# A decoder layer with retrieved experts: how many expert rows are gathered per group, and where two steps stand in their queues

## The chip, the cores and the metric

The kernel runs as one program on one NeuronCore of a Trainium2 chip. The metric is the device time of one execution in microseconds (us), the median of several runs. The engines are TensorE (PE, its weight loads PEld), VectorE (DVE), ScalarE (ACT), GpSimd (POOL) and SyncE (SP). Each runs its own queue in order. Engines wait for one another through semaphores, and transfers run on 16 DMA engines.

## What is computed

One decoder layer over 1024 tokens of width 1024. After RMSNorm, half of the heads run dilated-window attention and half run latent attention; their output is projected and added. Then comes the part that the change touches, a mixer over 16384 single-neuron experts:

```python
def peer(hn, w_pq, sub_keys, u_emb, v_emb):
    q = (t @ w_pq).reshape(-1, 8, 2, 128)
    sc = einsum('thpc,hpnc->thpn', q, sub_keys)
    vals, idx = top_k(sc, 16)                       # ranking
    cand = vals[:, :, 0, :, None] + vals[:, :, 1, None, :]
    best, flat = top_k(cand.reshape(..., 256), 16)
    expert = i1 * 128 + i2                          # 8 heads x 16 experts per token
    gate = softmax(best)
    act = gelu(einsum('td,thkd->thk', t, u_emb[expert]))
    out = einsum('thk,thkd->td', act * gate, v_emb[expert])
```

The layer's output is the final RMSNorm of the residual plus `out`.

## The kernel before

The stages follow one another: projection, attention, output projection, then `route` (ranking), `spread_gates` (gate tables) and `run_experts`.

**Two ways for the experts.** 576 tokens are computed densely: every expert's u is multiplied with every token, and the result is gated by a table that is zero where the expert was not chosen. The other 448 tokens are computed by gathering. They form 7 units of 64 tokens. For each unit the u rows of 128 tokens-by-slots are gathered by an indirect DMA into a ring of 4 tiles of 128x1024, and each tile costs one "dot" on DVE. Then v rows are gathered into a ring of 8 tiles. Four tiles make one "row sum" on PE (`sums`, L1921).

**Groups.** `run_experts` walks over 64 groups of two expert chunks each. On PE a group is `activations(g+1, 0)`, the first half of `out(g)`, `activations(g+1, 1)`, the second half of `out(g)`. I call an activation (48 matmuls, L1879) with the output half behind it (48 matmuls, L1895) a **half**. The output half is four fills of PSUM, and each fill needs the fill two before it to have been added to `acc` on DVE (`add`, L2084). 16 of the 128 chunks had their activations computed early, in `route`; chunk n is such a one where n % 8 is 3. So each group g with g % 4 == 0 has no second activation: I call it a **short group**.

**Where the row sums stand.** PE calls `catch_up(rows)` at four places of a group: behind the first activation (a), behind the first output half (b), behind the second activation (c), behind the second output half (d). At each it runs the row sums that the rows up to that number allow: all rows of the groups before, plus none, a quarter, a half, three quarters of this group's new rows, rounded down.

**The table of gathers.** `plan` sets how many dots and v rows each group gets. v rows of a unit may begin in the group after the one in which the unit's 64 dots are known to be done. POOL issues a group's u and v gathers in turn (L1844, L1852). A u gather waits for the dot four before it, a v gather for the row sum that frees its place. Before the change there are 9 dots a group up to group 9, then 8 dots and 8 v rows to group 54, 7 and 8 in group 55, and 80 v rows in groups 56 to 62.

**DVE in a group.** After each activation and its gelu on ACT (L1982), DVE runs `gated` (L2060), `split_u` (L2048), `split_w` (L2065) and then `add(g, 0)` or `add(g, 4)`. In the first half it also runs `split_v` (L2070), which the output half needs.

**Ranking's tail.** `route` goes over 8 heads. Beside the ranking it computes 16 early chunks. Each takes a transfer, a copy on ACT (L1178), a subtraction on POOL (`low`, L1294), 48 matmuls on PE (L1104) and a gelu on ACT (L1184). The last four chunks come with the last head.

Of the kernel before, what the change touches and what calls it, by code (L numbers as in the profile page):

```python
# [34 lines left out]
NC_ = sum(RUN)  # L35
NEXP = NKEY * NKEY
UNITS, UNIT, PIECES = 7, 64, 4
ROWS_A_GROUP, MOST_DOTS, LAST_ROWS = 16, 9, 16
T0 = UNITS * UNIT
TD = SEQ - T0  # L40
GT = (T0 + P - 1) // P
# [4 lines left out]
PER_HEAD, U_BUFS = 2, 2  # L46
# [937 lines left out]
def route(core, hn_hi, hn_lo, w_raw, keys, slotT, eid, eidT, sgate):  # L984
# [15 lines left out]
    with ExitStack() as ctx:  # L1000
# [172 lines left out]
        def _(act):  # L1173
            def copy_u(k):
                act.wait_ge(u_in, ONE + k * 16 + 16)
                if k >= U_BUFS:
                    act.wait_ge(act_done, ONE + k + 1 - U_BUFS)
                nc.scalar.activation(u_hi[:, k % U_BUFS, :], u_raw[:, :], ACT.Copy).then_inc(u_hi_ready, 1)  # L1178
# [63 lines left out]
            first_head()  # L1242
            for h in range(1, PH):
                head(h)
            k = 6 * PER_HEAD
            copy_u(k)
            copy_u(k + 1)
            gelu(k)
            gelu(k + 1)
            exponentials(PH)  # L1250
            copy_u(k + 2)
            copy_u(k + 3)
            gelu(k + 2)
            gelu(k + 3)
            for m in range(2):
                act.wait_ge(gelu_sent[m], ONE + 16 * PRE // 2)
            act.wait_ge(eidT_done, 1)
# [28 lines left out]
        @block.gpsimd  # L1286
        def _(pool):
            own = Own(pool, own_p)

            def low(k):  # L1290
                pool.wait_ge(u_hi_ready, ONE + k + 1)
                if k >= U_BUFS:
                    pool.wait_ge(act_done, ONE + k + 1 - U_BUFS)
                nc.gpsimd.tensor_tensor(u_lo[:, k % U_BUFS, :], u_raw[:, :], u_hi[:, k % U_BUFS, :].bitcast(f32), ALU.subtract  # L1294
                                        ).then_inc(u_lo_ready, 1)

            for h in range(PH):
                k = (h - 1) * PER_HEAD
                for j in range(PER_HEAD if h else 0):
                    low(k + j)  # L1300
                pool.wait_ge(keys_ranked, ONE + h + 1)
                pool.wait_ge(found_ready, ONE + h * NQ)
                near_sums(nc.gpsimd, own)
                pair_sums(nc.gpsimd, own, number, top_key)
                pool.sem_inc(number_ready, 1)
                for q in range(NQ):
                    n = h * NQ + q
                    pool.wait_ge(hit_ready, ONE + n * 2 + 2)
                    pool.wait_ge(summed, ONE + n * 2)
                    for z, src in ((0, near), (1, number)):  # L1310
                        own.mark(nc.gpsimd.tensor_tensor(
                            founds[z][:, :, :, :], hits[z][:, q % 2, :, :, :],
                            src[:, q * QT:(q + 1) * QT, :].rearrange("p i (c o) -> p i c o", o=1)
                            .to_broadcast([P, QT, (NN, NC_)[z], HALF]), ALU.mult))
                    own.sync()
                    pool.sem_inc(found_ready, 1)
                for j in range(PER_HEAD, 4 if h == PH - 1 else 0):
                    low(k + j)
                own.restart()

        @block.vector
# [132 lines left out]
class Lead:  # L1454
# [17 lines left out]
    def copy_u(self, nc, act, c):  # L1472
        act.wait_ge(self.u_in[c], 16)
        nc.scalar.activation(self.u_hi[:, c, :, :], self.u_raw[:, c, :].rearrange("p (j e) -> p j e", e=P),
                             ACT.Copy).then_inc(self.u_hi_ready, 1)
# [142 lines left out]
def plan(groups):  # L1618

    total = UNITS * UNIT
    turn, wrote = [], []
    u_by, v_by = [0], [0]
    while v_by[-1] < total:
        g, u, v = len(u_by), u_by[-1], v_by[-1]
        if len(turn) < UNITS and u >= (len(turn) + 1) * UNIT and len(wrote) >= PIECES * len(turn):
            turn.append(g)
        ready = min(sum(UNIT for t in turn if t < g) - v, UNIT - v % UNIT)
        nv = min(ready, LAST_ROWS if u == total and v % UNIT else 8)  # L1630
        nu = min(total - u, ROWS_A_GROUP - nv, MOST_DOTS)
        while len(wrote) * (UNIT // PIECES) < v + nv:
            wrote.append(g)
        u_by.append(u + nu)
        v_by.append(v + nv)
    spare = groups - len(u_by)
    assert spare >= 0
    return u_by + [total] * spare, v_by + [total] * spare, turn, wrote


def run_experts(core, eid, eidT, sgate, lead):
# [21 lines left out]
    with ExitStack() as ctx:  # L1663
# [378 lines left out]
        def _(dve):  # L2042
# [126 lines left out]
            for g in range(NG):  # L2169
# [7 lines left out]
                    coefficients(x)  # L2177
                some_dots(g, 2, 3)
                gated(g + 1, 0)
                split_u(g + 2, 0)  # L2180
                split_w(g + 1, 0)
                for x in closes(g):
                    close(x)
                add(g, 0)
                some_dots(g, 3, 4)
                add(g, 1)
                add(g, 2)
                some_dots(g, 4, 5)
                add(g, 3)
# [1 line left out]
                    take_coef(g, x)  # L2191
                some_dots(g, 5, 7)
                gated(g + 1, 1)
                split_u(g + 2, 1)
                split_w(g + 1, 1)
                for x in closes(g - 1):
                    mean(x, False)
                add(g, 4)
                some_dots(g, 7, 8)
                add(g, 5)  # L2200
                add(g, 6)
                some_dots(g, 8, 9)
                for x in closes(g - 2):
# [108 lines left out]
```

## Time and profile before

| | |
|---|---|
| median of 3 runs | 3306.6 us (3303.07 to 3311.08) |
| profiled execution | 3305.81 us, its span 3304.0 us |
| PE busy | 2975.8 us, 90% |
| DVE busy | 2220.1 us, 67% |
| POOL busy | 1264.4 us, 38% |
| ACT busy | 988.9 us, 30% |
| mean granted TensorE clock | 0.972 of full speed |

`run_experts` begins near 1399 us and is more than half of the span. The share of busy time of an engine is a mean over stages, so the stages have to be read one by one. Matmul ends are modelled in the trace; the starts of PE's instructions are what a length is taken from. The profiled execution lies 0.8 us below the median.

### The profile page before, as it was taken

The page shows a single profiled execution, that of the slowest core. Times are in us where ns is not written, and L with a number is a line of the kernel's source. Part 1 is how long each engine was busy: PE and PEld are TensorE (multiplying, and loading weights), DVE is VectorE, ACT ScalarE, POOL GpSimd, SP SyncE. Part 2 cuts the span into 40 slices and gives each one's busy share as a digit, 9 for nine tenths or more (in the row PEclk, how much of TensorE's full clock was granted, in tenths as well). Part 3 has the DMA queues.
Part 4 walks back from the last instruction along what each step waited for, and adds up shares of the span by engine and source line. Part 5 has one row for each costly group of instructions (what it writes and reads, how often), then busy time and mean ns, then how long its engine had stood idle before and what let it go on. Part 6 is the DMA issues. An engine that isn't in the chain of part 4 may idle for free.

```text
span 3304.0 us, 52758 instructions
## 1 busy us (share of the span) xinstructions
PE 2975.8 (90%) x19914; PEld 2435.1 (74%) x19914; DVE 2220.1 (67%) x5340; ACT 988.9 (30%) x1452; POOL 1264.4 (38%) x1088
## 2 busy tenths in 40 slices
PE   8997988997898666689999999999999999999997
PEld 4444666545777566688888888888889889888876
DVE  2223544336999889868887777778777777777435
ACT  2223655312222278722221222221222221222212
POOL 0000000001343400023357767767677666675241
PEclk9998999999999899999999999999999999999998
DMA  5213111112121126798799999999999999999684
GB/s 190 99 62 120 40 42 36 35 57 99 62 69 43 47 64 191 245 302 269 256 325 387 379 377 382 390 371 389 382 381 380 380 386 378 379 387 338 227 320 167
DMA packets 330177, 779.26 MB, mean 236 GB/s; under 512 B 45649, under 2 KB 147281, under 8 KB 328529
## 3 DMA queue, kind: packets, MB, share of 16 engines
q0 software_dynamic: 129024, 469.82, 37.8%
q1 hardware_dynamic: 178512, 288.92, 25.0%
q10 hardware_dynamic: 22400, 17.32, 1.6%
q8 instruction: 150, 2.46, 0.3%
q14 instruction: 91, 0.74, 0.1%
HBM read 699.42 MB, written 72.35 MB: 234 GB/s over the span
## 4 chain that ended last, share of the span: by engine, by line
PE 45%; DVE 9%; DMA 5%; issue 3%; ACT 1%; POOL 1%; SPq 0%; DVEq 0%; ACTq 0%
PE psum L1879 21%; PE psum L1895 19%; PE psum L1921 5%; DVE first L1564 4%; DMA u_ring<-u_rows,eid 3%; DVE one L1557 1%; DMA scr_g<-gates 1%; DVE acc L2084 1%; DVE u_lo L2048 1%; POOL v_ring L1852 1%; ACT u_hi L1976 1%; DVE second L1567 1%; DMA v_ring<-v_rows,eidT 1%; DMA v_raw<-v_rows 0%; DVE w_lo L2065 0%
## 5 line engine op out<-in xcount | busy, mean ns | idle before, releaser
L1852 POOL DMA_INDIRECT v_ring<-v_rows,eidT x448 | 598.2, 1335 | 413.0 <-PE psum L1921 303.4
L1844 POOL DMA_INDIRECT u_ring<-u_rows,eid x448 | 513.1, 1145 | 293.4 <-DVE dots L2092 187.7
L2092 DVE CUSTOM_DVE_ANT_0 u_ring<-u_ring,rows 128x1024 f32<-128x1024 f32 x448 | 545.0, 1218 | 98.1 <-DMA u_ring<-u_rows,eid 97.2
L1879 PE MATMUL psum<-hn_hi_e,u_hi 128*128 128x288 f32 x1792 | 531.2, 296 | 8.5 <-SPq L108 5.0
L1879 PE MATMUL psum<-hn_lo_e,u_hi 128*128 128x288 f32 x1792 | 528.8, 295 | 0.0
L1879 PE MATMUL psum<-hn_hi_e,u_lo 128*128 128x288 f32 x1792 | 528.5, 295 | 0.0
L1895 PE MATMUL psum<-w_hi,v_hi 128*128 128x288 f32 x2048 | 464.9, 309 | 69.6 <-DVE acc L2084 59.0
L2084 DVE TENSOR_TENSOR acc<-psum,acc 128x576 f32<-128x576 f32 x504 | 380.1, 755 | 138.8 <-PE psum L1895 128.5
L1895 PEld LDWEIGHTS psum<-w_hi,v_hi 128*128 128x128 f32 x2048 | 333.9, 193 | 171.0 <-issue 91.0
L1895 PE MATMUL psum<-w_lo,v_hi 128*128 128x288 f32 x2048 | 446.8, 300 | 0.0
L1895 PE MATMUL psum<-w_hi,v_lo 128*128 128x288 f32 x2048 | 446.1, 300 | 0.0
L1879 PEld LDWEIGHTS psum<-hn_hi_e,u_hi 128*128 128x128 f32 x1792 | 338.2, 189 | 14.9 <-issue 14.9
L1895 PEld LDWEIGHTS psum<-w_hi,v_lo 128*128 128x128 f32 x2048 | 338.2, 193 | 0.0
L1895 PEld LDWEIGHTS psum<-w_lo,v_hi 128*128 128x128 f32 x2048 | 338.1, 193 | 0.0
L1879 PEld LDWEIGHTS psum<-hn_lo_e,u_hi 128*128 128x128 f32 x1792 | 338.0, 189 | 0.0
L1879 PEld LDWEIGHTS psum<-hn_hi_e,u_lo 128*128 128x128 f32 x1792 | 337.6, 188 | 0.0
L1982 ACT ACTIVATE psum<-psum 128x576 f32<-128x576 f32 x112 | 71.1, 635 | 872.1 <-PE psum L1879 872.1
L1993 ACT ACTIVATE v_hi<-v_raw 128x1024 fp32r<-128x1024 f32 x128 | 128.8, 1054 | 407.4 <-PE psum L1895 395.7
L2060 DVE TENSOR_TENSOR w<-psum,w 128x576 f32<-128x576 f32 x112 | 84.8, 757 | 232.3 <-ACT psum L1982 219.6
L1921 PE MATMUL psum<-v_ring,strip 128*32 128x512 f32 x1792 | 216.9, 602 | 10.4 <-DMA v_ring<-v_rows,eidT 10.4
L473 PE MATMUL psum<-w_in,hT 128*128 128x512 f32 (+1 forms) x512 | 211.7, 575 | 0.0
L1582 PE MATMUL psum<-second,first 128*128 128x128 f32 x1152 | 148.0, 283 | 70.7 <-DVE second L1567 70.7
(238 smaller groups left out, 4192.8 us busy)
## 6 DMA issues: line engine op xcount, KB each, us to landing
v_raw<-v_rows SPq DMA_DIRECT2D x128, 512.0 KB, 7.1
u_raw<-uT SPq DMA_DIRECT2D x112, 512.0 KB, 8.1
w<-scr_g SPq DMA_DIRECT2D x128, 288.0 KB, 5.8
scr_g<-gates SPq DMA_DIRECT2D x3, 8192.0 KB, 30.6
scr_m<-st_m SPq DMA_DIRECT2D x8, 1024.0 KB, 4.0
w_raw<-in_w_pq SPq DMA_DIRECT2D x8, 1024.0 KB, 6.6
u_raw_r<-uT SPq DMA_DIRECT2D x16, 512.0 KB, 3.5
scr_g<-gates ACTq DMA_DIRECT2D x1, 7680.0 KB, 36.9
```

Of the source, the lines that this page charges most:

```text
L473: last = nc.tensor.matmul(ps[:, 2 + c, 0:width(c)], hT[:, k, j, :], w_in[:, j, c * BANK:c * BANK + width(c)], start=j == 0, stop=j == KD - 1)
L1564: nc.vector.tensor_scalar(first[:, b, t, :], iota_f[:, :], flat[:, 0, at:at + 1], flat[:, 2, at:at + 1], ALU.is_equal, ALU.mult).then_inc( ...
L1582: last = nc.tensor.matmul(slot, first[:, b, t, :], second[:, b, t, :], start=True, stop=True)
L1844: pool.indirect_dma_start(u_ring[:, n % U_RING, :], None, core.i["u_rows"], bass.IndirectOffsetOnAxis(eid[:, x // 2, x % 2, k:k + 1], 0)). ...
L1852: pool.indirect_dma_start(v_ring[:, m % V_RING, :], None, core.i["v_rows"], bass.IndirectOffsetOnAxis(eidT[:, x // 2, col:col + 1], 0)).th ...
L1879: last = nc.tensor.matmul(ps[:, a, 0:COLS], x[:, c, j, :], y[:, j, a * COLS:(a + 1) * COLS], start=m == 0, stop=m == len(terms) - 1)
L1895: last = nc.tensor.matmul(ps[:, OUT_AT + F % OUT_PAIRS * 2 + a, 0:COLS], x[:, c, f * P:(f + 1) * P], y[:, b, c, a * COLS:(a + 1) * COLS], ...
L1921: last = nc.tensor.matmul(ps[k * WIDE:(k + 1) * WIDE, SUM_AT + half, :], strip[:, p % 2, at:at + WIDE], v_ring[:, n % V_RING, half * BANK: ...
L1993: nc.scalar.activation(v_hi[:, c, :], v_raw[:, c, :], ACT.Copy).then_inc(v_hi_ready, 1)
L2060: nc.vector.tensor_tensor(half, ps[:, 0:ACTS, 0:COLS], half, ALU.mult).then_inc(w_ready, 1)
L2084: nc.vector.tensor_tensor(into, ps[:, at:at + 2, 0:COLS], into, ALU.add).then_inc(added, 1)
L2092: nc.vector.tensor_tensor_reduce(out=u, in0=u, in1=rows[:, x % 2, :], scale=1.0, scalar=0.0, op0=ALU.mult, op1=ALU.add, accum_out=dots[:, ...
```

## The change

The table of gathers becomes: 10 dots a group in groups 1 to 8; then 8 dots with 7 v rows (8 in the first group of each unit's v rows) in groups 9 to 54; then, with no dots left, 16 v rows a group, 120 of them in groups 55 to 62. In groups whose predecessor has no v rows (0 to 9), `add(g, 0)`, `add(g, 1)`, `add(g, 4)` and `add(g, 5)` move ahead of `split_w`, the first of each pair ahead of `split_u`. In `route` POOL runs the last four `low` in a row ahead of the last head's `near_sums`, and ACT runs its last four chunks ahead of the last head's exponentials.

```diff
-ROWS_A_GROUP, MOST_DOTS, LAST_ROWS = 16, 9, 16
+U_ROWS, MOST_DOTS, LAST_ROWS = 8, 10, 16
...
-            k = 6 * PER_HEAD
-            copy_u(k)
-            copy_u(k + 1)
-            gelu(k)
-            gelu(k + 1)
+            copy_u(6 * PER_HEAD)
+            copy_u(6 * PER_HEAD + 1)
+            for k in range(6 * PER_HEAD, PRE):
+                gelu(k)
+                if k + 2 < PRE:
+                    copy_u(k + 2)
             exponentials(PH)
-            copy_u(k + 2)
-            copy_u(k + 3)
-            gelu(k + 2)
-            gelu(k + 3)
...
-                for j in range(PER_HEAD if h else 0):
+                for j in range(0 if h == 0 else PER_HEAD if h < PH - 1 else PRE - k):
                     low(k + j)
...
-                for j in range(PER_HEAD, 4 if h == PH - 1 else 0):
-                    low(k + j)
...
-        nv = min(ready, LAST_ROWS if u == total and v % UNIT else 8)
-        nu = min(total - u, ROWS_A_GROUP - nv, MOST_DOTS)
+        nv = min(ready, LAST_ROWS if u == total else 7 if v % UNIT else 8)
+        nu = min(total - u, U_ROWS if nv else MOST_DOTS)
...
                 gated(g + 1, 0)
+                alone = not g or v_by[g - 1] == 0
+                if alone:
+                    add(g, 0)
                 split_u(g + 2, 0)
+                if alone:
+                    add(g, 1)
                 split_w(g + 1, 0)
                 for x in closes(g):
                     close(x)
-                add(g, 0)
+                if not alone:
+                    add(g, 0)
                 some_dots(g, 3, 4)
-                add(g, 1)
+                if not alone:
+                    add(g, 1)
```

The second half of a group is changed in the same way, with `add(g, 4)` and `add(g, 5)`.

On PE, group 11 before: a row sum (L1921) stands between each activation (L1879) and its output half (L1895).

```order
L1879 MATMUL psum<-hn_hi_e,u_hi 128x288
...
L1921 MATMUL psum<-v_ring,strip 32x512 x8
L1895 MATMUL psum<-w_hi,v_hi 128x288 x2
...
L1879 MATMUL psum<-hn_hi_e,u_hi 128x288
...
L1921 MATMUL psum<-v_ring,strip 32x512 x8
L1895 MATMUL psum<-w_hi,v_hi 128x288 x2
...
```

Group 11 now (L1874, L1916 and L1890 are the same three statements):

```order
L1874 MATMUL psum<-hn_hi_e,u_hi 128x288
...
L1890 MATMUL psum<-w_hi,v_hi 128x288 x2
...
L1916 MATMUL psum<-v_ring,strip 32x512 x8
L1874 MATMUL psum<-hn_hi_e,u_hi 128x288
...
L1890 MATMUL psum<-w_hi,v_hi 128x288 x2
...
L1916 MATMUL psum<-v_ring,strip 32x512 x8
```

Both row sums moved behind the output half. With 7 rows a group the quarter points fall differently in each of four groups, and a group has one of these four forms (a, b, c, d as above, the number of row sums at each):

| form | a, b, c, d | ordinary groups among 11 to 54 | short groups among them |
|---|---|---|---|
| P | 1, 0, 0, 1 | 7 | 2 |
| Q | 0, 1, 0, 1 | 8 | 2 |
| R | 0, 0, 1, 0 | 6 | 4 |
| S | 1, 0, 1, 0 | 12 | 3 |

Before the change all 44 of these groups have form S.

On DVE, the first half of a group without v rows, before: three steps and then the first addition.

```order
L2060 TENSOR_TENSOR w<-psum,w 128x576
L2048 TENSOR_TENSOR u_lo<-u_raw,u_hi 128x1024
L2065 TENSOR_TENSOR w_lo<-w,w_hi 128x576
L2084 TENSOR_TENSOR acc<-psum,acc 128x576
L2092 ISA u_ring,dots<-u_ring,rows 128x1024
```

And now:

```order
L2055 TENSOR_TENSOR w<-psum,w 128x576
L2079 TENSOR_TENSOR acc<-psum,acc 128x576
L2043 TENSOR_TENSOR u_lo<-u_raw,u_hi 128x1024
L2079 TENSOR_TENSOR acc<-psum,acc 128x576
L2060 TENSOR_TENSOR w_lo<-w,w_hi 128x576
```

The two additions moved ahead, one of them past two steps.

On POOL, the last head before: two subtractions, the sums of the last head, and two subtractions at the end.

```order
L1294 TENSOR_TENSOR u_lo_r<-u_raw_r,u_hi_r 128x1024 x2
L1281 TENSOR_TENSOR near<-top_key 128x8x8
...
L1311 TENSOR_TENSOR found<-hit,near 128x640
L1311 TENSOR_TENSOR found<-hit,number 128x1600
L1294 TENSOR_TENSOR u_lo_r<-u_raw_r,u_hi_r 128x1024 x2
L93 ISA
```

And now all four stand ahead of the sums:

```order
L1291 TENSOR_TENSOR u_lo_r<-u_raw_r,u_hi_r 128x1024 x4
L1278 TENSOR_TENSOR near<-top_key 128x8x8
...
L1308 TENSOR_TENSOR found<-hit,near 128x640
L1308 TENSOR_TENSOR found<-hit,number 128x1600
L93 ISA
```

## Rows read from the trace of the kernel before

**Rows 1.** Windows; columns: stretch, length, each engine's busy us, clock, DMA share, GB/s.

```profile
1458.00:1694.00 236.00, 214.23 (x1540) 207.37 (x1539) 195.32 (x289) 50.94 (x64) 93.75 (x79) 0.99 0.80 267
1780.00:3011.00 1231.00, 1200.58 (x8935) 1061.22 (x8935) 953.67 (x1391) 275.97 (x346) 854.10 (x673) 0.98 1.00 381
3011.00:3263.00 252.00, 239.21 (x1800) 202.09 (x1802) 116.33 (x153) 50.87 (x65) 94.40 (x90) 0.99 0.77 280
```

**Rows 2.** Timeline, PE, a half of group 13; columns: start us, us, instruction.

```profile
1780.23 0.29 PE L1879 MATMUL psum<-hn_hi_e,u_hi 128*128 128x288 f32 x1
...
1786.67 1.92 PE L1921 MATMUL psum<-v_ring,strip 128*32 128x512 f32 x16
...
1788.52 0.53 PE L1895 MATMUL psum<-w_hi,v_hi 128*128 128x288 f32 x2
...
1795.03 0.29 PE L1879 MATMUL psum<-hn_hi_e,u_hi 128*128 128x288 f32 x1
```

**Rows 3.** Timeline, PE, the first half of group 10.

```profile
1693.91 0.29 PE L1879 MATMUL psum<-hn_hi_e,u_hi 128*128 128x288 f32 x1
...
1700.27 0.43 PE L1895 MATMUL psum<-w_hi,v_hi 128*128 128x288 f32 x2
...
1704.71 0.53 PE L1895 MATMUL psum<-w_hi,v_hi 128*128 128x288 f32 x2 [1.09 <-DVE acc L2084]
...
1708.20 0.29 PE L1879 MATMUL psum<-hn_hi_e,u_hi 128*128 128x288 f32 x1
```

**Rows 4.** Timeline, DVE, in the same half of group 10.

```profile
1701.21 0.76 DVE L2060 TENSOR_TENSOR w<-psum,w 128x576 f32<-128x576 f32 x1 [1.29 <-ACT psum L1982]
1702.10 1.22 DVE L2048 TENSOR_TENSOR u_lo<-u_raw,u_hi 128x1024 fp32r<-128x1024 f32 x1
...
1703.91 0.75 DVE L2084 TENSOR_TENSOR acc<-psum,acc 128x576 f32<-128x576 f32 x1
```

**Rows 5.** Timeline, PE, group 59, a row sum behind an output half.

```profile
3145.43 1.92 PE L1921 MATMUL psum<-v_ring,strip 128*32 128x512 f32 x16
...
3147.28 0.40 PE L1879 MATMUL psum<-hn_hi_e,u_hi 128*128 128x288 f32 x1
```

**Rows 6.** Timeline, short group 12: POOL, DVE, PE.

```profile
1763.11 0.94 POOL L1844 DMA_INDIRECT u_ring<-u_rows,eid  x1 [0.30 <-issue]
...
1770.99 1.23 DVE L2092 CUSTOM_DVE_ANT_0 u_ring<-u_ring,rows 128x1024 f32<-128x1024 f32 x1 [1.30 <-DMA u_ring<-u_rows,eid]
...
1775.42 0.54 PE L1895 MATMUL psum<-w_hi,v_hi 128*128 128x288 f32 x2 [2.64 <-DVE acc L2084]
```

**Rows 7.** Windows: short group 12, then groups 59, 60 (short) and 61.

```profile
1752.60:1780.20 27.60, 24.96 (x178) 21.52 (x177) 22.95 (x35) 5.86 (x7) 21.26 (x17) 0.94 1.03 408
3130.60:3164.10 33.50, 33.50 (x257) 27.12 (x256) 15.20 (x21) 9.97 (x12) 11.86 (x12) 1.00 0.78 287
3164.10:3199.00 34.90, 28.71 (x212) 21.26 (x208) 15.48 (x19) 6.21 (x8) 16.10 (x16) 0.96 0.99 360
3199.00:3232.90 33.90, 33.90 (x260) 27.48 (x256) 11.96 (x15) 6.11 (x8) 16.21 (x16) 0.99 0.79 285
```

**Rows 8.** Timeline, group 2, dots alone: PE, DVE, PE.

```profile
1472.33 0.29 PE L1879 MATMUL psum<-hn_hi_e,u_hi 128*128 128x288 f32 x1
...
1476.63 1.22 DVE L2070 TENSOR_TENSOR v_lo<-v_raw,v_hi 128x1024 fp32r<-128x1024 f32 x1
...
1478.69 0.43 PE L1895 MATMUL psum<-w_hi,v_hi 128*128 128x288 f32 x2
```

**Rows 9.** Timeline, the end of ranking: POOL, DVE, PE, and DVE's first step of the next stage.

```profile
1123.56 1.64 POOL L1281 TENSOR_TENSOR near<-top_key 128x64 f32<-128x64 f32 x8 [1.42 <-DVEq L1431]
...
1153.58 0.38 DVE L1412 CAST slot<-key_i 128x80 f32<-128x80 int32 x2
...
1164.18 0.60 PE L1163 MATMUL psum<-ident,eid_f 128*128 128x128 f32 x4
...
1172.22 0.69 DVE L1548 CAST iota_gb<-iota 128x1024 bf16<-128x1024 f32 x1 [18.27 <-PEq L108]
```

More of the change, by code:

```diff
@@ L2193, in _ @@
                 gated(g + 1, 1)
+                if alone:
+                    add(g, 4)
                 split_u(g + 2, 1)
+                if alone:
+                    add(g, 5)
                 split_w(g + 1, 1)
@@ L2197, in _ @@
                     mean(x, False)
-                add(g, 4)
+                if not alone:
+                    add(g, 4)
                 some_dots(g, 7, 8)
-                add(g, 5)
+                if not alone:
+                    add(g, 5)
                 add(g, 6)
```

## The prediction

> **What bounds the kernel now.** I read the windows by stage first, because the shares on the page mix them. From 1780 to 3011 us, the stage with dots and v rows, PE is busy 1200.6 of 1231.0 us and the DMA share is 1.00 at 381 GB/s [rows 1]. So two things could set the pace there, and the timeline of PE has to say which. In an ordinary half it runs without a gap: activation from 1780.23, row sum from 1786.67, output from 1788.52, the next activation at 1795.03 [rows 2]. That is 6.44 + 1.85 + 6.51 = 14.80 us, and the half behind it is the same. PE is the bound, not the DMA engines. The number of matmuls is unchanged, so the time can only change through PE's waits.
>
> Where PE waits, it is for DVE's additions. The first half of group 10 has no row sum between activation and output. It takes 1708.20 - 1693.91 = 14.29 us although it has 1.85 us less to do: PE stops 1.09 us ahead of the third fill, and about 0.4 us in smaller stops [rows 3]. The reason is DVE's order: `gated` at 1701.21, `split_u`, `split_w`, and only at 1703.91 the addition that frees the PSUM for the third fill [rows 4]. A row sum ahead of the output half gives DVE just that time. So a row sum there costs 14.80 - 14.29 = 0.5 us, not 1.85. **This is the number on which the forecast rests.** A row sum behind the output half covers nothing: it costs 1.85 us [rows 5], about 1.9 with the slower restart.
>
> The short groups are the exception. Group 12 takes 27.6 us [rows 7] against 6.4 + 4 x 3.25 + 2 x 1.85 = 23.1 of work. Its last two fills wait for DVE: a dot waits 1.30 us for a u row that was issued at 1763.11, and PE's fill comes at 1775.42 after 2.64 us [rows 6]; the mean clock of the group is 0.94 [rows 7]. The eleven short groups among 12 to 52 take 27.9 us on average by the starts of their first activations.
>
> **The dots-alone stage.** It fills 1458 to 1694 us [rows 1]. Each half takes 14.3 us, for the reason of [rows 3]. With the additions ahead, the 1.47 us of waits in a half go, since the addition is done 1.81 us earlier (the span from `split_u` to `add`, 1702.10 to 1703.91) [rows 4]. But the tenth dot takes some of it back. In the first half the output waits for `split_v`: now it ends near 1477.85, and the output starts at 1478.69, 6.36 us after the activation began at 1472.33 [rows 8]. Slack 0.84. One more dot (1.14 from start to start) stands ahead of it, and PE arrives 1.47 sooner relative to DVE: 0.84 - 1.14 - 1.47 = -1.8, a new wait. A group becomes 2 x (6.36 + 6.48) + 1.8 = 27.5 instead of 28.6: -1.1 each in five ordinary groups. The two short groups lose about 1.5 each (the 1.81 of `add(g, 4)` less some lateness). Group 1 loses 1.1, group 9 nothing. Group 10 gets form P: +1.9. Sum: -5.5 - 3.0 - 1.1 + 1.9 = **-7.7**. Bounds: -17 if the tenth dot finds room, +2 if it costs 1.14 in full.
>
> **The mixed stage, groups 11 to 54.** All 44 groups now have form S, and 33 of them are ordinary ones of 29.6 us. By [rows 2, 3, 5]:
> P = 14.8 + 14.3 + 1.9 = 31.0, or +1.4; 7 groups, +9.8.
> Q = 2 x 14.3 + 2 x 1.9 = 32.4, or +2.8; 8 groups, +22.4.
> R = 14.3 + 14.8 = 29.1, or -0.5; 6 groups, -3.
> S = +0; 12 groups.
> Ordinary groups together +29.2. Ten row sums leave this stage for the end, but 23 of those that stay stand where they cover nothing.
>
> In a short group the end is set by DVE, from the first `gated` on. Form R lacks the wait for one row sum's fill (-0.6) and the late u row (-1.3): -1.9. Q and P end with a bare sum, +1.9, less about 0.5 of the dot's wait: +1.4. S is +0.7, as in groups 40 and 44 the sixth u row is queued behind a v row that waits for the sum at a. That is 4 x -1.9 + 4 x 1.4 + 3 x 0.7, or **0**. Bounds: 27.9 could fall to 24.9 if the late row (1.3) and the slow clock (1.7) both went, -33 for the eleven; +2 each, +22. I take 0, as the 1.4 us and more that PE waits for DVE's order stay in all of them, and the clock fell there. Together **+29**.
>
> **The end, groups 55 on.** Before, groups 55 to 62 took 252 us [rows 1]. Now seven of eight have 16 rows. Ordinary: 33.5, or 33.9 behind a short one; short: 34.9, as its row sums wait for the ring of eight [rows 7]. So 3 x 33.5 + 2 x 33.9 + 2 x 34.9 + 29.8 for group 58 and 1.0 for coefficients and a `close` = 268.9: **+17**. Bounds +12 and +22 (the short ones wait 8 us now; 3 more or less each).
>
> **Ranking.** POOL starts the last head's `near_sums` at 1123.56. It now runs two more `low` first. Each waits for a transfer, ACT's copy and PE's chunk before; laid out by the row starts, the fourth ends near 1136.5, so the sums are 13 us later. The exponentials come after the last gelu, near 1147 instead of 1133. From there DVE and POOL need as long as before: the last row on DVE moves from 1153.6 to about 1160.8. But the transposes had waited for PE's last chunk until 1164.18, and that now ends near 1144. Transposes at 1161 let ACT end at 1165. Then SP is last, with eight small transfers (5.4 us to issue, some 2 to land): 1168.4 in place of 1170.6. The next stage starts at 1170 instead of 1172.2 [rows 9]: **-2**. Bounds -5 and +3. If the cover of PE's chunk were gone without the gain, the 7 us on DVE would show.
>
> The first group's gain is swallowed: group 1's output waits for v rows of the dense path that land at a time set by the transfers.
>
> **Sum.** -2 - 7.7 + 29 + 0 + 17 = +36 on a span of 3304.0. The profiled execution is 0.8 below the median, so the median goes from 3306.6 to about **3343 us**.
>
> **Rivals.** (1) The DMA engines set the pace of the mixed stage, and the change makes it *faster*. For it speaks the share of 1.00. 37 of 336 v gathers leave groups 13 to 54, 0.524 MB each (128x1024 f32), 19.4 MB, which at 381 GB/s is 51 us. It decides if PE's halves lengthen or shorten with the gathers. Time: 3306.6 - 51 + 17 - 10 = 3263. Against it: gapless halves of 14.80 us [rows 2], and 408 GB/s in a short group [rows 7], so 381 is no ceiling. The Trainium skill (DMA: Bandwidth & Descriptors, Where 436 GB/s comes from) says that for HBM to SBUF the HBM side, about 358 GB/s a core, binds. By that rule the mixed stage would be bound by its transfers. The rows speak against that figure, at 381 and 408. Chance 0.12.
>
> (2) Fewer gathers make u rows land in time, and the short groups keep the fast clock: -33 in place of 0, 3310 us. Speaks for it: the dot's wait in [rows 6]. Against it: without the 1.30 the fill would still come 1.3 us late. Chance 0.08.
>
> (3) A u row queued behind a v row that waits for a late row sum holds DVE. In form R, u row 7 stands behind the v row that waits for the sum at c. If it lands as late as in [rows 6], 7.9 us after its issue, DVE is 2.1 us late in the next group, ten times: +21, 3364 us. I think that such a row lands sooner, since POOL stood still before it. Chance 0.08.
>
> **Chances and range.** My forecast 0.70, the rest 0.02. Its own range is 3318 to 3366, from the bounds above. With (2) and (3) the range is 3300 to 3372, which leaves out (1). About 0.2%, 6.6 us, is what a measurement can tell from no change. Faster 0.13, same 0.08, slower 0.79.
>
> **What would show it.** Halves of 14.3 us with a wait of about 1.1 for `acc` wherever no row sum stands between activation and output, with v rows under way; a row sum behind an output at 1.85; period of four groups near 119 to 121 us where Q and P stand; groups 55 to 62 at 269; groups of 27.5 in the dots-alone stage. Wrong: bare halves of 13 us in the mixed stage, or ordinary covered halves shorter than 14.8. Then the reading of [rows 3] or the bound is wrong.

## The result, and the profile after

The changed kernel takes 3381.4 us (median of 4 runs, 3375.4 to 3384.0) against 3308.1 us of the kernel before in the same session: 1.022 times as long, 95% interval 1.020 to 1.025. It is slower, as forecast, but by 73 us instead of 36, and 3381 lies above the range, which ended at 3372. The profiled execution has a span of 3380.8 us, 76.8 more than before.

Windows of the changed kernel, by the same stages as [rows 1] (columns as there):

```profile
1448.00:1684.50 236.50, 217.18 (x1584) 211.90 (x1583) 205.02 (x307) 51.53 (x64) 117.72 (x93) 0.99 0.86 298
1776.00:3072.30 1296.30, 1203.79 (x8790) 1061.62 (x8789) 947.94 (x1384) 273.66 (x343) 753.35 (x634) 0.98 0.93 346
3072.30:3338.90 266.60, 255.79 (x1908) 205.76 (x1906) 109.92 (x143) 53.48 (x67) 116.96 (x116) 0.98 0.88 314
```

Groups 13 to 54 take 1296 us instead of 1231, with PE busy for nearly the same time (1204 and 1201 us), and the DMA share fell from 1.00 to 0.93. So PE waits there, and the DMA engines are less busy than before.

From here on I measure a group from the start of its first activation to the next group's. All group times are worked out so, from the timelines of PE.

| stretch, us after minus before | forecast | measured |
|---|---|---|
| ahead of the first changed step | 0 | -4.3 |
| ranking's end | -2 | -3.1 |
| gate tables and groups 0 to 10 | -7.7 | 0.0 |
| groups 11 to 54, ordinary, forms P, Q, R | +29 | +27.5 |
| groups 11 to 54, ordinary, form S | 0 | +21.4 |
| groups 11 to 54, short | 0 | +19.7 |
| groups 55 to the end | +17 | +15.6 |
| sum | +36 | +76.8 |

So the account is right where it rests on measured halves. It fails in the forms S and short, which I had put at zero, and by 7.7 us in groups 0 to 10. The groups of the costliest kinds, from the page of the kernel before and then of the changed one (line, engine, operation, count; busy us, mean ns; idle us ahead of them, and its releaser):

```profile
L1852 POOL DMA_INDIRECT v_ring<-v_rows,eidT x448 | 598.2, 1335 | 413.0 <-PE psum L1921 303.4
L2092 DVE CUSTOM_DVE_ANT_0 u_ring<-u_ring,rows 128x1024 f32<-128x1024 f32 x448 | 545.0, 1218 | 98.1 <-DMA u_ring<-u_rows,eid 97.2
```

```profile
L1847 POOL DMA_INDIRECT v_ring<-v_rows,eidT x448 | 524.9, 1172 | 556.7 <-PE psum L1916 444.2
L2087 DVE CUSTOM_DVE_ANT_0 u_ring<-u_ring,rows 128x1024 f32<-128x1024 f32 x448 | 544.5, 1219 | 162.7 <-DMA u_ring<-u_rows,eid 161.3
L1890 PE MATMUL psum<-w_hi,v_hi 128*128 128x288 f32 x2048 | 469.4, 311 | 130.8 <-DVE acc L2079 92.1
```

POOL's v gathers wait 141 us longer for row sums, and DVE's dots wait 64 us longer for u rows. These are sums over the whole kernel; in groups 11 to 54 alone, by the timelines, it is 149 and 55 us. There are fewer gathers to make in these groups, and yet they came later.

**A bare half, as forecast.** PE in group 11 of the changed kernel, to be held against [rows 3] and [rows 5]:

```profile
1715.62 0.40 PE L1874 MATMUL psum<-hn_hi_e,u_hi 128*128 128x288 f32 x1
...
1722.08 0.43 PE L1890 MATMUL psum<-w_hi,v_hi 128*128 128x288 f32 x2
...
1726.53 0.53 PE L1890 MATMUL psum<-w_hi,v_hi 128*128 128x288 f32 x2 [1.10 <-DVE acc L2079]
...
1730.11 1.92 PE L1916 MATMUL psum<-v_ring,strip 128*32 128x512 f32 x16
...
1731.97 0.40 PE L1874 MATMUL psum<-hn_hi_e,u_hi 128*128 128x288 f32 x1
```

The half takes 14.49 us with a stop of 1.10, and the row sum behind it 1.86. Form P measured +1.2 a group, Q +2.7, R -0.5 (forecast +1.4, +2.8, -0.5).

**What the forecast missed.** POOL, DVE and PE where group 21 (form R) passes into group 22 (form S):

```profile
2032.30 0.94 POOL L1839 DMA_INDIRECT u_ring<-u_rows,eid  x1 [0.69 <-DVE dots L2087]
2043.13 1.55 POOL L1847 DMA_INDIRECT v_ring<-v_rows,eidT  x1 [9.88 <-PE psum L1916]
2044.98 0.94 POOL L1839 DMA_INDIRECT u_ring<-u_rows,eid  x1 [0.30 <-issue]
2046.23 1.11 POOL L1839 DMA_INDIRECT u_ring<-u_rows,eid  x1 [0.30 <-issue]
```

```profile
2054.36 1.22 DVE L2087 CUSTOM_DVE_ANT_0 u_ring<-u_ring,rows 128x1024 f32<-128x1024 f32 x1 [5.76 <-DMA u_ring<-u_rows,eid]
```

```profile
2060.00 0.50 PE L1890 MATMUL psum<-w_hi,v_hi 128*128 128x288 f32 x2 [2.38 <-DVE v_lo L2065]
2064.08 0.53 PE L1890 MATMUL psum<-w_hi,v_hi 128*128 128x288 f32 x2 [0.66 <-DVE acc L2079]
```

v row 6 waits 9.88 us for the row sum at c. u row 7 stands behind it in POOL's queue and is issued at 2044.98. Its dot starts at 2054.36, 9.4 us later, after DVE has waited 5.76 us for the row. So `split_v` is late, and PE waits 2.38 and 0.66 us. That is the third rival of the prediction, in its own words. I had given it 0.08.

### The profile page after: what moved, and what is told of

The parts are those of the page before. It is cut to its first block, busy times and chain, and to the rows that moved or that the text cites. A ratio compares the mean times of both kernels' runs of the same rounds, so it can differ in the third digit from the quotient of the medians.

```text
span 3380.8 us, 52758 instructions
## 1 busy us (share of the span) xinstructions
PE 2988.7 (88%) x19914; PEld 2434.0 (72%) x19914; DVE 2208.1 (65%) x5340; ACT 990.5 (29%) x1452; POOL 1200.1 (35%) x1088
## 4 chain that ended last, share of the span: by engine, by line
PE 37%; DVE 12%; DMA 8%; issue 4%; POOL 2%; ACT 1%; SPq 0%; DVEq 0%; POOLq 0%; ACTq 0%
PE psum L1874 17%; PE psum L1890 15%; DMA u_ring<-u_rows,eid 5%; PE psum L1916 5%; DVE first L1559 4%; DVE acc L2079 2%; POOL v_ring L1847 2%; DVE one L1552 1%; DVE u_ring L2087 1%; DVE u_lo L2043 1%; DMA scr_g<-gates 1%; DMA v_ring<-v_rows,eidT 1%; ACT u_hi L1971 1%; POOL u_ring L1839 1%; DVE w_lo L2060 1%
## 5 line engine op out<-in xcount | busy, mean ns | idle before, releaser
L1847 POOL DMA_INDIRECT v_ring<-v_rows,eidT x448 | 524.9, 1172 | 556.7 <-PE psum L1916 444.2
L1839 POOL DMA_INDIRECT u_ring<-u_rows,eid x448 | 523.8, 1169 | 310.8 <-DVE dots L2087 202.1
L1890 PE MATMUL psum<-w_hi,v_hi 128*128 128x288 f32 x2048 | 469.4, 311 | 130.8 <-DVE acc L2079 92.1
L1874 PE MATMUL psum<-hn_hi_e,u_hi 128*128 128x288 f32 x1792 | 533.9, 298 | 8.3 <-SPq L108 5.0
L1874 PE MATMUL psum<-hn_lo_e,u_hi 128*128 128x288 f32 x1792 | 528.4, 295 | 0.0
L1874 PE MATMUL psum<-hn_hi_e,u_lo 128*128 128x288 f32 x1792 | 528.1, 295 | 0.0
L1890 PEld LDWEIGHTS psum<-w_hi,v_hi 128*128 128x128 f32 x2048 | 335.6, 194 | 218.8 <-DVE acc L2079 116.9
L1890 PE MATMUL psum<-w_hi,v_lo 128*128 128x288 f32 x2048 | 447.8, 301 | 0.0
L1890 PE MATMUL psum<-w_lo,v_hi 128*128 128x288 f32 x2048 | 447.5, 301 | 0.0
L1874 PEld LDWEIGHTS psum<-hn_hi_e,u_hi 128*128 128x128 f32 x1792 | 337.3, 188 | 42.3 <-issue 42.3
L1890 PEld LDWEIGHTS psum<-w_lo,v_hi 128*128 128x128 f32 x2048 | 339.3, 194 | 0.0
L1890 PEld LDWEIGHTS psum<-w_hi,v_lo 128*128 128x128 f32 x2048 | 338.5, 194 | 0.0
L1874 PEld LDWEIGHTS psum<-hn_lo_e,u_hi 128*128 128x128 f32 x1792 | 337.4, 188 | 0.0
L1874 PEld LDWEIGHTS psum<-hn_hi_e,u_lo 128*128 128x128 f32 x1792 | 337.2, 188 | 0.0
L1916 PE MATMUL psum<-v_ring,strip 128*32 128x512 f32 x1792 | 219.4, 608 | 12.8 <-DMA v_ring<-v_rows,eidT 12.7
```

The source lines that it names most:

```text
L1839: pool.indirect_dma_start(u_ring[:, n % U_RING, :], None, core.i["u_rows"], bass.IndirectOffsetOnAxis(eid[:, x // 2, x % 2, k:k + 1], 0)). ...
L1847: pool.indirect_dma_start(v_ring[:, m % V_RING, :], None, core.i["v_rows"], bass.IndirectOffsetOnAxis(eidT[:, x // 2, col:col + 1], 0)).th ...
L1874: last = nc.tensor.matmul(ps[:, a, 0:COLS], x[:, c, j, :], y[:, j, a * COLS:(a + 1) * COLS], start=m == 0, stop=m == len(terms) - 1)
L1890: last = nc.tensor.matmul(ps[:, OUT_AT + F % OUT_PAIRS * 2 + a, 0:COLS], x[:, c, f * P:(f + 1) * P], y[:, b, c, a * COLS:(a + 1) * COLS], ...
L1916: last = nc.tensor.matmul(ps[k * WIDE:(k + 1) * WIDE, SUM_AT + half, :], strip[:, p % 2, at:at + WIDE], v_ring[:, n % V_RING, half * BANK: ...
```

## Experiments

Each time is the median of 4 to 10 runs, and each ratio is to runs of the kernel before on the same chip (3305 to 3310 us). The profiles are read from one execution each.

### The parts of the change

`table_alone` is the kernel before with the first hunk and the hunk of `plan` alone:

```diff
-ROWS_A_GROUP, MOST_DOTS, LAST_ROWS = 16, 9, 16
+U_ROWS, MOST_DOTS, LAST_ROWS = 8, 10, 16
...
-        nv = min(ready, LAST_ROWS if u == total and v % UNIT else 8)
-        nu = min(total - u, ROWS_A_GROUP - nv, MOST_DOTS)
+        nv = min(ready, LAST_ROWS if u == total else 7 if v % UNIT else 8)
+        nu = min(total - u, U_ROWS if nv else MOST_DOTS)
```

> The kernel before with nothing changed but the table of gathers. It splits the +73 us. In the two traces the ranking's end gives 3 us (of the 10 us that run_experts starts earlier, 4.3 were there before the first changed step), and group 2, dots alone, went from 28.6 to 27.4 us. With the old order of the additions I expect such a group at 28.9 us (14.3 a half, and the tenth dot 0.3 more than the slack of 0.84), so five such groups and two short ones cost some 9 us more than in the changed kernel. Expected: 3381 + 3 + 9, about 3393 us. If the early additions are what hurts, it comes out below 3375.

Measured: 3395.7 us, ratio 1.025 (1.023 to 1.028). `old_table` is the changed kernel with these hunks undone.

> The changed kernel with the table of before (9 dots, then 8 and 8, 80 v rows at the end); ranking's end and the early additions stay. If the table alone costs, this is faster than before: 3 us from ranking; seven ordinary dots-alone groups at 2 x (6.36 + 6.48) + 0.63 of a wait for v_lo = 26.3 us in place of 28.6, 16 us; two short ones 1 us each. Expected 3308 - 21, about 3287 us. The rival, that the early additions hurt, has it above 3308.

Measured: 3285.7 us, ratio 0.993 (0.991 to 0.996). Both came within 3 us of what was expected. The table costs it all; the early additions and ranking's end gain. An ordinary dots-alone group takes 28.8 us in `table_alone`, 27.4 in the changed kernel and 26.3 in `old_table`: the additions give 1.4 with ten dots and 2.3 with nine.

Ranking's end can be read from all traces at once. From the last `found` on POOL ahead of the changed steps to DVE's first step of the next stage it takes 64.1 us before and 64.2 in `table_alone`, and 60.9 to 61.2 in each of the twelve kernels with the new end. Before, and then after (the row of before that answers to the last one is in [rows 9]):

```profile
1108.12 1.29 POOL L1311 TENSOR_TENSOR found<-hit,near 128x640 f32<-128x640 bf16 x1 [11.57 <-DVE expert L1385]
```

```profile
1103.81 1.29 POOL L1308 TENSOR_TENSOR found<-hit,near 128x640 f32<-128x640 bf16 x1 [11.56 <-DVE expert L1380]
...
1164.89 0.69 DVE L1543 CAST iota_gb<-iota 128x1024 bf16<-128x1024 f32 x1 [8.77 <-PEq L108]
```

The 4.3 us between the two `found` rows lie ahead of every changed step. That start varies from kernel to kernel in no order (1103.3 to 1109.6; `table_alone`, with the old end, has 1109.6), so the 4.3 us are no gain of the change.

### The order of the gathers

`u_ahead` leaves the table and the row sums alone. On POOL it holds back each v gather that waits for a row sum, and the v gathers behind it, until two more u gathers are issued:

```diff
+            held, ahead = [], 2
...
                         gather_u(u)
-                        u += 1
+                        u, ahead = u + 1, ahead + 1
                     else:
-                        gather_v(v)
+                        if v >= V_RING and v % STRIPS == 0:
+                            ahead = 0
+                        held.append(v)
                         v += 1
+                    while held and (ahead >= 2 or u == NS):
+                        gather_v(held.pop(0))
```

> The changed kernel, but on POOL a v row that waits for a row sum (every fourth) is issued only after the next two u rows, which in the changed kernel stand behind it. Same table, same row sums at the same places. Theory of the queue: the dots that wait for rows in the groups behind form R and in the short groups get them in time; of the 21 us that form S lost and the 20 us of the short groups about 30 go, 3350 us, and DVE's idle time for u_ring falls from 162 to under 110 us. Theory of the bare halves: the loss sits in DVE's order where no row sum covers it, the dots' waits are hidden anyway: 3375 us or more.

Measured: 3349.1 us, ratio 1.011 (1.009 to 1.014). On its page:

```profile
L1847 POOL DMA_INDIRECT v_ring<-v_rows,eidT x448 | 513.1, 1145 | 290.5 <-PE psum L1921 164.4
L2092 DVE CUSTOM_DVE_ANT_0 u_ring<-u_ring,rows 128x1024 f32<-128x1024 f32 x448 | 543.6, 1219 | 86.4 <-DMA u_ring<-u_rows,eid 84.5
```

Groups 11 to 54 take 1320.4 us, 32.3 more than before and 36.3 less than in the changed kernel. Of the 36.3, 23.6 come from the short groups, which are now at 303.2 for all eleven (before 307.1), and 12.7 from the ordinary ones. Q and R stay within 0.1 us in all, and P but for groups 37 and 41 (1.3 and 0.7 more). So the order in the queue is shown as the cause of 38 of the 41 us that forms S and short had cost. Ordinary form S keeps +6.8 (3.7 of it in group 17), and no run says why.

`one_row` reduces this to the rival as I had put it:

```diff
                     else:
+                        if v % STRIPS == 0 and v + 1 == v_by[g] and u < u_by[g]:
+                            gather_u(u)
+                            u += 1
                         gather_v(v)
                         v += 1
```

> The changed kernel with one edit, in the ten groups of form R: u row 7 is issued ahead of v row 6, which waits for the row sum at c, instead of behind it. Everything else, the other three forms too, stays. This is the third rival of the prediction and nothing else. If that one row is what holds DVE, the excess of form S behind R (groups 17, 22, 26, 31, 35, 49: 19 us over 29.6) goes, and of the short groups 20 to 32 perhaps a few us: about 3360 us, and u_ahead's other 10 us are those of the forms Q, P and S. If the next group's first u row, which still stands behind v row 6, is as late, nothing is gained: 3375 us or more.

Measured: 3369.4 us, ratio 1.020 (1.017 to 1.022), between the two. Ordinary form S falls from +21.4 to +12.2 us, the short groups stay (326.6 against 326.8). POOL and DVE at the same place:

```profile
2036.26 0.94 POOL L1839 DMA_INDIRECT u_ring<-u_rows,eid  x1 [1.77 <-DVE dots L2091]
2044.38 1.55 POOL L1847 DMA_INDIRECT v_ring<-v_rows,eidT  x1 [7.18 <-PE psum L1920]
2046.23 0.94 POOL L1839 DMA_INDIRECT u_ring<-u_rows,eid  x1 [0.31 <-issue]
```

```profile
2056.10 1.23 DVE L2091 CUSTOM_DVE_ANT_0 u_ring<-u_ring,rows 128x1024 f32<-128x1024 f32 x1 [3.01 <-DMA u_ring<-u_rows,eid]
```

u row 7 is early now, and DVE waits for the next group's u row 0, which still stands behind v row 6. The dot of that row starts 9.9 us after the row's issue. So the named row was a bit less than half of the loss of form S (9.2 of 21.4). The short groups lose by the same queue too, but not by that row: with it alone put right they gain 0.2 us, with `u_ahead` 23.6.

### Row sums at a and c alone

```diff
                 for x in turns(g):
                     turn_coef(g, x)
-                catch_up(old + new // 4)
...
                 out(g, range(FILLS // 2, FILLS))
-                catch_up(old + new * 3 // 4)
```

> The changed kernel with row sums only at a and c: the calls at b and d are gone, and what they ran comes at the next a or c. Same table and gathers. Form P becomes 1,0 and the three others 1,1, so only one half in eight is bare. Theory of the bare halves (all of the loss comes from them): the forms P and Q fall from +1.4 and +2.8 to -0.5 and 0, the short groups and form S go back to 0 too, and 3381 - 30 - 41 - 5 is left, about 3305 us. Theory of the queue: 3381 - 30 - 5, about 3346 us, since the v row behind which u7 stands waits for the same row sum at c, and form S behind it keeps its +3.6 a group.

Measured: 3540.7 us, ratio 1.068 (1.065 to 1.071). Both theories were far off. The seven P groups did fall to 29.0 us on average, below before, as bare halves say, but each ordinary Q group rose to 44.5 to 47.4 us. POOL, DVE and PE in the first of these, group 11:

```profile
1713.56 1.24 POOL L1839 DMA_INDIRECT u_ring<-u_rows,eid  x1 [2.23 <-issue]
1727.54 1.54 POOL L1847 DMA_INDIRECT v_ring<-v_rows,eidT  x1 [12.74 <-PE psum L1916]
1729.39 0.94 POOL L1839 DMA_INDIRECT u_ring<-u_rows,eid  x1 [0.30 <-issue]
```

```profile
1736.31 1.23 DVE L2085 CUSTOM_DVE_ANT_0 u_ring<-u_ring,rows 128x1024 f32<-128x1024 f32 x1 [6.50 <-DMA u_ring<-u_rows,eid]
```

```profile
1738.27 0.85 PE L1890 MATMUL psum<-w_hi,v_hi 128*128 128x288 f32 x2 [6.05 <-DVE acc L2077]
```

A row sum one activation later holds a v row, that holds a u row, that a dot, that an addition, and that PE's fill, behind which the next row sum stands. In this group the ring stops PE for 6.05 and 6.03 us, once in each half. The halves are 7.7 and 8.2 us longer than 14.8; behind each stop the granted clock was 0.50 for some 3.3 us:

```profile
1738.00:1741.30 3.30, 3.03 (x12) 3.04 (x13) 2.11 (x4) 0.00 (x0) 0.34 (x1) 0.50 1.02 408
```

`covered_u_ahead` is meant to open the ring:

> The changed kernel with row sums only at a and c, as in the run `covered` (3541 us), and with the u rows ahead of the waiting v row, as in `u_ahead` (3349 us). Theory: in `covered` PE's row sum, DVE's addition, the dot, the u row and the v row ahead of it wait for one another in a ring, six of the forms Q and S losing 15 us each; with the u rows ahead that ring is open. What is then left against `u_ahead` is that bare halves are gone: P at 29.1 and Q, R, S at 29.6, short groups as there, so groups 11 to 54 take about 978 + 303 = 1281 us in place of 1320: 3349 - 39 = 3310 us. Rival: the v rows that are issued later hold the row sums themselves, and it is 3340 us or more.

Measured: 3367.2 us, ratio 1.018 (1.016 to 1.020). The ordinary groups came as expected to within 11 us (988.8 in place of 978; Q 30.2 to 31.3 instead of 45), so there the ring is open. The short groups did not: 341.7 instead of 303 us. In these the dots still wait for u rows (group 48: 1.4, 1.1 and 4.6 us in a row) and PE behind them for an addition (5.8 us). Why these rows are late was not told apart. The time is where the rival put it, above 3340 us, but not for its reason: in groups 11 to 54 of this trace no row sum waits for a v row.

### The order of DVE's steps

`bare_early` extends the early additions of the change to each half in which it leaves PE bare:

```diff
-                alone = not g or v_by[g - 1] == 0
+                alone = bare(g, 0)
...
                 gated(g + 1, 1)
+                alone = g % 4 == 0 or bare(g, 1)
                 if alone:
                     add(g, 4)
```

`bare(g, c)` is true where `catch_up` runs no row sum at a (c = 0) or at c (c = 1).

> The changed kernel with the additions early in every half that has no row sum between activation and output, and in the second half of every short group. A bare half takes 14.3 us because the first addition stands behind split_u and split_w on DVE. If that is the reason, it now takes 6.36 + 6.49 = 12.85 us: form P 14.80 + 12.85 + 1.85 = 29.5 (was 31.1), Q 2 x 12.85 + 3.7 = 29.4 (was 32.2 to 32.7), R 27.65 (was 29.2). P, Q and R together 12 + 25 + 9 = 46 us less, short groups some 25 less, 3381 - 71 = 3310 us. Two things may take part of it back: v_lo has only 0.84 us of slack in the half behind (0.6 in each of 14 groups, 9 us), and the queue of gathers is still as it was and now meets a faster PE (form S behind R keeps its +3.6, and more). Rival: PE's stop in a bare half has another cause than DVE's order, and P, Q, R stay within 0.3 us.

Measured: 3326.8 us, ratio 1.006 (1.004 to 1.007). PE and DVE in group 10:

```profile
1704.19 0.29 PE L1874 MATMUL psum<-hn_hi_e,u_hi 128*128 128x288 f32 x1
...
1710.55 0.43 PE L1890 MATMUL psum<-w_hi,v_hi 128*128 128x288 f32 x2
...
1717.04 1.92 PE L1916 MATMUL psum<-v_ring,strip 128*32 128x512 f32 x16
...
1718.89 0.40 PE L1874 MATMUL psum<-hn_hi_e,u_hi 128*128 128x288 f32 x1
```

```profile
1711.49 0.76 DVE L2055 TENSOR_TENSOR w<-psum,w 128x576 f32<-128x576 f32 x1 [1.16 <-ACT psum L1977]
1712.34 0.76 DVE L2079 TENSOR_TENSOR acc<-psum,acc 128x576 f32<-128x576 f32 x1
1713.02 1.22 DVE L2043 TENSOR_TENSOR u_lo<-u_raw,u_hi 128x1024 fp32r<-128x1024 f32 x1
```

The bare half is 12.85 us, to the hundredth what was expected; of the 35 in groups 11 to 54, 30 take 12.8 to 12.95 us and the others up to 13.6. P is at 29.5, Q at 29.6 and R at 27.65 us (28.3 where a unit closes). The shortfall against 3310 sits in the forms that had been blamed on the queue: ordinary S still costs +23 us (groups 22, 26, 35 and 53 by 3.4 to 5.6 each), and the short groups gained 13 us where 25 were expected. With both edits:

> `bare_early` with the u rows ahead of the waiting v row. Where the queue is one cause and DVE's order the other, the two gains add: u_ahead was 32 us below the changed kernel, so 3310 - 32 = 3278 us, 24 us above `short_early` (3254), which has the table of before. If both edits remove the same wait, they don't add and it stays within 10 us of `bare_early`.

Measured: 3292.1 us, ratio 0.996 (0.994 to 0.998). That is 14 us above the 3278 expected, which were counted from an expected 3310 for `bare_early`; from its measured 3326.8 they would be 3295. In groups 11 to 54 the two gains are 36.3 and 52.3, and together 87.8: they add, so they are two causes.

### A better version

`short_early` has the table of before and the early additions in dots-alone groups, and in the second half of every short group:

```diff
                 gated(g + 1, 1)
+                alone = alone or g % 4 == 0
                 if alone:
                     add(g, 4)
```

> The run `old_table` (3286 us: table of before, the new end of ranking, the early additions in groups 0 to 9), with the early additions in the second half of every short group too. There PE waits 2.8 us for the addition of fill 5 (group 12: output half of 11.1 us in place of 6.5). If DVE's order is the reason, that wait goes: 3 us in each of twelve groups, 3250 us. If DVE is simply full in a short group (8 additions, 8 dots and 7 splits and gates, 23.8 us, for 23.1 of PE's), the gain is given back in the next half, as a later v_lo: 3275 us or more.

Measured: 3254.0 us, ratio 0.984 (0.983 to 0.986): 51 us faster than the kernel before and 127 faster than the changed one. Short group 12, windows, `old_table` and then `short_early`:

```profile
1727.20:1755.05 27.85, 25.03 (x179) 21.59 (x177) 22.98 (x35) 5.85 (x7) 21.09 (x17) 0.94 1.03 406
```

```profile
1729.20:1754.33 25.13, 23.68 (x178) 20.07 (x177) 21.00 (x33) 5.86 (x7) 19.14 (x15) 1.00 1.03 408
```

PE's wait ahead of the third fill of the second output half falls from 2.82 to 1.45 us, and the mean granted clock of the group is 1.00 in place of 0.94. The eleven short groups of the mixed stage fall from 307.1 to 274.0 us, and the ordinary ones rise by 8.7.

> `short_early` with the u rows ahead of the waiting v row as well. With the table of before the dots wait 1.3 to 1.5 us for a row once in a short group and nowhere else where it matters, so the queue is worth at most 1.5 us in each of eleven groups: 16 us below `short_early` if the order theory holds, nothing if the row's wait only takes the place of DVE's wait for PE.

Measured: 3253.4 us, ratio 0.985 (0.983 to 0.987), the same time. With the table of before the order of the gathers is worth nothing: short groups 6.3 us less, ordinary ones 3.2 more. `uneven` (from `short_early_u_ahead`) and `seven_nine` (from `short_early`) give the short groups fewer dots:

```diff
-        nu = min(total - u, ROWS_A_GROUP - nv, MOST_DOTS)
+        nu = min(total - u, (5 if g % 4 == 0 else 9) if nv else MOST_DOTS)
```

> `short_early_u_ahead` with 5 dots in a short group and 9 in each of the three others of the mixed stage, 32 in four groups as before. DVE's work in a short group falls from 23.8 to 20.1 us, below PE's 23.1. If a full DVE is what keeps short groups at 27.9 us, each comes near 24 and this is 20 us faster than `short_early_u_ahead`. Against it: the ninth dot takes 1.14 us where v_lo has 0.84 of slack, 0.3 us in 33 groups, 10 us back. If the order alone was the reason, it is 10 us slower.

> `short_early` (3254 us) with 7 dots in a short group and 9 in the group two behind it; the order on POOL is that of the changed kernel. Short groups take 24.9 us there, against 23.1 of PE's work. `uneven` (5 and 9, 9, 9, u rows ahead) brought them to 23.2 but cost 67 us in the ordinary groups, where a u row is issued when the dot four before it has ended, then lands 7 to 9 us later while the v rows of the same burst are under way. If that cost comes from the ninth dot in the group right behind the short one, this version keeps most of the gain: 24.9 - 1.1 in eleven groups, 3242 us. If every group with nine dots and eight v rows pays (some 4 us, eleven times), it is near 3290.

In `seven_nine` the 5 and the 9 are `(7, 8, 9, 8)[g % 4]`. Measured: `uneven` 3310.7 us (ratio 1.001, 1.000 to 1.002), `seven_nine` 3292.2 us (0.996, 0.994 to 0.997). `uneven` was 57 us slower than its base, where 20 faster or 10 slower had been expected; `seven_nine` came at the 3290 expected where every group with nine dots pays. The short groups reach 23.2 us in `uneven`, PE's work of 23.1 and no more, and 23.9 in `seven_nine`. But a ninth dot beside eight v rows costs 79 us more than before in `uneven`'s ordinary groups, and in `seven_nine` 41 more than in `short_early`, nearly all of it in the groups with nine dots. DVE waits there for rows again: group 17 of `uneven`, POOL and DVE.

```profile
1882.08 1.04 POOL L1839 DMA_INDIRECT u_ring<-u_rows,eid  x1 [0.30 <-issue]
```

```profile
1891.48 1.22 DVE L2092 CUSTOM_DVE_ANT_0 u_ring<-u_ring,rows 128x1024 f32<-128x1024 f32 x1 [4.89 <-DMA u_ring<-u_rows,eid]
```

The dot of that row starts 9.4 us after its issue, too. Which other transfers the row meets in the DMA queues was not told apart.

## Why the prediction was right in part and wrong in size

**The bound.** That PE's waits and not the DMA engines set the pace held. Covered halves without a stop are 14.8 us as in [rows 2]. Rival (1) is out: with 37 v gathers fewer in the stage no covered half became shorter, and short group 12 of `short_early` moved 408 GB/s, above the 346 of the changed kernel's stage.

**Bare halves.** Right: 13.9 to 14.6 us, most of them 14.4 to 14.6, against 14.3 by [rows 3], 1.86 for a row sum behind an output against [rows 5], P, Q and R together +27.5 against +29. The reading of [rows 4], that the stop comes from DVE's order, is shown by `bare_early`: 12.85 us.

**Form S, "+0; 12 groups".** Wrong, +21.4. The step that failed is the one that put rival (3) aside: "I think that such a row lands sooner, since POOL stood still before it." I took 7.9 us from issue to dot from [rows 6] and expected less. The view of DMA issues, which gives the median time in us from issue to landing, would have said that 7.9 is the usual time. Its row in the kernel before, and then in the changed one:

```profile
u_ring<-u_rows,eid POOLq DMA_INDIRECT x448, 8.1
```

```profile
u_ring<-u_rows,eid POOLq DMA_INDIRECT x448, 7.7
```

Behind the v row that had waited, the u row 7 of the ten groups of form R lands 5.4 to 10.0 us after its issue, 7.8 in the mean, and the u row 0 of the next group 6.4 to 11.2 us, 9.3 in the mean. So the pause of POOL won nothing for the first row, and the next one, in the burst that follows the pause (a gather each 1.2 us), came later than usual. The rival's mechanism was right. That its 21 us meet the 21.4 of form S is in part luck: the row that it named accounts for 9.2 of them (`one_row`), and the queue's whole price was 36.3 (`u_ahead`). Of the 21.4, 19.4 stand in the ordinary groups right behind a form R.

**Short groups, "0".** Wrong, +19.7, near the bound of +22 that I had written and then took as an end of the range. Form R did gain where it could (groups 16, 48 and 52 by 1.9 to 2.6), Q and P lost what bare sums cost and more, and S lost 5.9 and 8.8 in groups 40 and 44, where I had put 0.7 for a u row behind the v row that waits for the sum at a. That v row waits only 1.1 and 1.7 us there. Both groups stand behind a form R, whose v row 6 waits 9.89 and 10.01 us. POOL ahead of group 44, and in it:

```profile
2730.54 0.94 POOL L1847 DMA_INDIRECT v_ring<-v_rows,eidT  x1 [10.01 <-PE psum L1916]
...
2745.33 1.67 POOL L1847 DMA_INDIRECT v_ring<-v_rows,eidT  x1 [1.70 <-PE psum L1916]
```

With the u rows ahead, all eleven come to -4. The whole excess goes with the order in the queue. In a short group a dot already waits 1.30 us for a row, and PE 2.64 us behind it ([rows 6]), so a row that comes later still can lengthen the group at once. The forecast had that row and did not carry it over.

**Dots alone.** Forecast -7.7, measured 0.0. Ordinary groups -4.6 against -5.5: a group takes 27.42 with a wait of 1.68 for `v_lo` (forecast 27.5 and 1.8; [rows 8] shows none). PE in group 2:

```profile
1464.64 0.29 PE L1874 MATMUL psum<-hn_hi_e,u_hi 128*128 128x288 f32 x1
...
1472.85 0.50 PE L1890 MATMUL psum<-w_hi,v_hi 128*128 128x288 f32 x2 [1.68 <-DVE v_lo L2065]
```

The two short ones gained nothing (forecast -3): with nine dots they do gain 1.5 and 1.2 (`old_table`), so the tenth takes it back. Group 9, put at nothing, cost +2.7: the first v rows come a group earlier now, and it has a row sum, dots that wait up to 2.7 us for rows, and a stop of 1.68 us on PE. Group 1 was put at -1.1; the gate tables and groups 0 and 1 together came to -0.3.

**Ranking.** -3.1 against -2, inside -5 to +3, and by the steps laid out. With the 4.3 us added that the run was ahead, the fourth `low` ends at 1137.4 (forecast 1136.5), DVE's last row is at 1160.0 (1160.8), the transposes at 1160.6 (1161) and the next stage at 1169.2 (1170).

**The end.** +15.6 against +17, in part by luck. The short groups 56 and 60 take 33.2 and 31.9 us instead of 34.9, and group 62 takes 36.5 instead of 33.5: PE waits 3.05 us there for a v row.

**The range.** It was formed from one cost at a time. The rival at +21 and the short groups' bound at +22 are the same queue, so they come together: 3343 + 21 + 22 = 3386. Taken so, the range would have reached the 3381 that was measured. And the 0.08 rested on a guess against [rows 6] and against the median of 8.1 us in the kernel before. One sign failed as well: four groups were to take 119 to 121 us, and they take 118 to 129.

## What to carry to other kernels

When a change moves the step that frees a buffer, look at what is queued behind the transfer that waits for the buffer, not only at who needs the buffer. Follow the ring to its end (row sum, v row, u row, dot, addition, fill), since a delay that returns to its own start is paid in each round, as `covered` showed. Before a row is said to land sooner or later than another, read the median of all landings of its kind. Two bounds that rest on the same resource have to be added in the range.

## What the runs showed of the hardware

An indirect gather of 128x1024 f32 has a record of 0.94 us on POOL in the median, but its data lands 7.7 us after the issue in the median of the changed kernel, and a dot that waits for it in a burst of gathers starts 9.4 us after its issue in the changed kernel (group 21) and 9.9 us in `one_row` (group 22). The Trainium skill (Perfetto Trace Analysis, DMA Instruction — SWDGE (GPSIMD)) says that the record of such a transfer ends when its descriptors are written and not when the data is there. The trace agrees: 0.94 us against 7.7.

A stop of 2.82 us in short group 12 of `old_table` was followed by a granted clock of 0.60 from 1750.2 to 1753.0 and 0.70 to 1755.0, after 1.00 ahead of the stop. With a stop of 1.45 us in its place (`short_early`) the group's clock was 1.00, and it gained 2.7 us, of which 1.4 are the shorter wait. The stops of 6 us in `covered` were followed by 0.50, which is the lower of the two levels of the clock (1.2 GHz, against 2.4 at 1.00); 0.60 and 0.70 are means of stretches with a part at each.
